# Loading experts' weights in 16 KB runs: the contraction index of each half matrix renamed

## The reference

```
t = RMSNorm(x) * ffn_norm_g                      # 256 x 1024
comb = softmax over the top 4 of 32 router logits # 256 x 32
for e in range(32):
    g = min(t @ w_gate[e] + b_gate[e], 7)
    u = clip(t @ w_up[e] + b_up[e], -7, 7)
    act = (u + 1) * (g * sigmoid(1.702 * g))
    out += comb[:, e] * (act @ w_down[e] + b_down[e])
```

## Time and profile before

| what | value |
|---|---|
| median of 3 runs | 1172.27 us |
| profiled execution: span, first to last instruction | 1169.7 us |
| TensorE matmul busy | 1102.9 us (94%) |
| TensorE weight load busy | 463.3 us (40%) |
| VectorE busy | 281.6 us (24%) |
| ScalarE busy | 190.4 us (16%) |
| bytes moved by DMA | 432.55 MB, 116,942 packets |
| mean DMA rate over the span | 370 GB/s |
| mean granted TensorE clock | 0.989 |

### The profile page before, as it was taken

The page is one execution under the profiler, slowest core; times in us unless marked ns, Lnnn a source line. Parts: engine busy times, 40 slices in busy tenths (PEclk is TensorE's granted clock), DMA queues, the critical chain, the costliest instruction groups (busy, mean ns, idle before and its releaser), DMA issues.

```text
span 1169.7 us, 13269 instructions
## 1 busy us (share of the span) xinstructions
PE 1102.9 (94%) x5385; PEld 463.3 (40%) x5385; DVE 281.6 (24%) x632; ACT 190.4 (16%) x361; POOL 62.6 (5%) x58
## 2 busy tenths in 40 slices
PE   6998998999999999999999999999999999999998
PEld 3787995333333333333333333333333333333332
DVE  4978664111111111111111111111111111111112
ACT  3645632100110010001000100001000100010000
POOL 0194120000000000000000000000000000000000
PEclk9989998999999999999999999999999999999999
DMA  8612478799999999999999999999999999999996
GB/s 314 256 73 108 171 295 334 293 402 409 409 409 409 410 409 409 409 410 410 409 409 410 410 409 410 409 410 410 409 409 410 410 410 409 410 410 409 409 409 259
DMA packets 116942, 432.55 MB, mean 370 GB/s; under 512 B 5557, under 2 KB 6106, under 8 KB 116922
## 3 DMA queue, kind: packets, MB, share of 16 engines
q1 hardware_dynamic: 116634, 431.60, 93.3%
q10 hardware_dynamic: 288, 0.67, 0.2%
HBM read 431.21 MB, written 1.05 MB: 370 GB/s over the span
## 4 chain that ended last, share of the span: by engine, by line
PE 48%; DMA 41%; DVE 7%; ACT 2%; SPq 1%; issue 1%; DVEq 0%; ACTq 0%
DMA ring<-in_exp_w_up 41%; PE ps L752 27%; PE ps L711 5%; PE ps L759 3%; PE ps L717 3%; PE ps L724 2%; PE ps L490 2%; PE ps L492 2%; PE ps L491 2%; DVE ring_r L1071 1%; DMA ring<-in_w_in 1%; SPq L434 1%; ACT ring_r L812 1%; DVE arena L1140 1%; DVE arena L1126 1%; PE ps L777 1%
## 5 line engine op out<-in xcount | busy, mean ns | idle before, releaser
L752 PE MATMUL ps<-ring,arena 128*64 128x512 f32 x3072 | 685.9, 594 | 32.5 <-DMA ring<-in_exp_w_gate 28.0
L752 PEld LDWEIGHTS ps<-ring,arena 128*64 128x64 f32 x3072 | 218.9, 137 | 486.8 <-issue 414.5
L1315 DVE TENSOR_SCALAR arena<-ps 128x512 f32<-128x512 f32 x32 | 22.1, 692 | 507.6 <-PE ps L752 507.6
L759 PE MATMUL ps<-arena 128*64 128x512 f32 x384 | 102.9, 614 | 0.3 <-issue 0.3
L1325 DVE TENSOR_SCALAR arena<-ps 128x512 f32<-128x512 f32 x32 | 22.1, 692 | 244.4 <-PE ps L752 244.4
L969 ACT COPY arena<-ps 128x512 f32<-128x512 f32 x32 | 18.8, 587 | 333.9 <-PE ps L711 333.9
L724 PE MATMUL ps<-arena 64*128 64x512 f32 x264 | 65.6, 615 | 0.8 <-ACT arena L975 0.8
L967 ACT ACTIVATE arena<-arena 128x512 f32<-128x512 f32 x32 | 20.1, 630 | 280.7 <-DVE arena L1315 280.7
L490 PE MATMUL ps<-ring_r 128*128 128x256 f32 (+1 forms) x192 | 61.1, 318 | 4.2 <-DVE ring_r L1071 2.4
L711 PE MATMUL ps<-arena 128*64 128x512 f32 x264 | 64.0, 607 | 0.8 <-DVE arena L1261 0.8
L975 ACT COPY arena<-ps 128x512 f32<-128x512 f32 x32 | 18.8, 586 | 249.0 <-PE ps L752 249.0
(11 more groups left out here) (185 smaller groups left out, 637.6 us busy)
## 6 DMA issues: line engine op xcount, KB each, us to landing
ring<-in_exp_w_gate SPq DMA_DIRECT2D x64, 2048.0 KB, 23.5
ring<-in_exp_w_up SPq DMA_DIRECT2D x64, 2048.0 KB, 23.7
ring<-in_exp_w_down SPq DMA_DIRECT2D x64, 2048.0 KB, 23.7
ring<-in_w_in SPq DMA_DIRECT2D x8, 2048.0 KB, 9.4
ring<-in_w_out SPq DMA_DIRECT2D x2, 2048.0 KB, 7.8
xt<-in_x SPq DMA_DIRECT2D x4, 512.0 KB, 6.9
ring<-in_pool_up SPq DMA_DIRECT2D x1, 2048.0 KB, 7.9
ring<-in_attn_up SPq DMA_DIRECT2D x1, 2048.0 KB, 8.6
```

Of the source, the lines that this page charges most:

```text
L752: last = mm(ps[BLOCK * half:BLOCK * (half + 1), bank, :], src[:, c, k % 2, :], slot(n)[:, c, HALF * half:HALF * (half + 1)], start=False, ...
L759: mm(ps[BLOCK * half:BLOCK * (half + 1), bank, :], this_e[:, buf, k, :], bias_rows[:, HALF * half:HALF * (half + 1)], start=True, stop=False)
L1315: v.tensor_scalar(g1, ps[:, 4, :], LIMIT, None, ALU.min).then_inc(g_ready, 1)
```

## The change

The contraction index of each half matrix is renamed: within a half of 512 rows, row 4 * p + c now belongs to partition p, block c. A partition's four rows are then neighbours in memory, one run of 16 KB. The bytes, the pieces, the slots, their order and their waits stay. To match it, VectorE writes `h2` and `act_out` with the same permutation of columns: it reads them in order, and writes neighbouring elements 128 elements (512 bytes) apart. Four of the `h2` writes and 32 of the `act_out` writes are concerned. The gain in the new order is loaded from HBM by one more DMA on ACT's queue (256 runs of 16 bytes), on a semaphore of its own, for which VectorE waits once before the loop. The router's part (`x2T`, `rw`, with the gain from `cols`) keeps the old order.

```diff
+        gain = sb("gain", [P, 2, 4])
...
+        gain_in = sem("gain_in")
...
-                        w = A[name][0].rearrange("e (c p) n -> p e c n", p=P)
+                        w = A[name][0].rearrange("e (h p c) n -> p e h (c n)", h=2, p=P)
...
-                            src = w[:, bass.ds(step * UNROLL + j, 1), 4 * half:4 * half + 4, :]
-                            src = src.rearrange("p e c n -> p (e c) n")
-                            sp.dma_start(slot(n), src).then_inc(slot_in[ORDER[n % SLOTS]], 16)
+                            src = w[:, bass.ds(step * UNROLL + j, 1), half:half + 1, :]
+                            src = src.rearrange("p e h n -> p (e h n)")
+                            sp.dma_start(ring[:, ORDER[n % SLOTS], :], src).then_inc(slot_in[ORDER[n % SLOTS]], 16)
...
             act.dma_start(con[:], consts).then_inc(con_in, 16)
+            act.dma_start(gain[:], A["ffn_norm_g"].rearrange("l (h p c) -> p (l h) c", h=2, p=P)).then_inc(gain_in, 16)
...
-                    v.tensor_scalar(h2[:, t, part_cols], xt[:, t, part_cols], rstd[:, t:t + 1], None,
+                    v.tensor_scalar(h2[:, t, part_cols].rearrange("q (c p) -> q p c", c=4),
+                                    xt[:, t, part_cols].rearrange("q (p c) -> q p c", c=4), rstd[:, t:t + 1], None,
                                     ALU.mult).then_inc(h2_ready, 1)
...
-                gain = cols[:, R_FFNG:R_FFNG + NC].rearrange("p (h c) -> p c h", h=2)
                 v.tensor_tensor(h_in[:, buf], ps[:, 6, :].rearrange("p (c h s) -> p c h s", c=4, h=2),
-                                wide(gain, [P, 4, 2, BLOCK], 3), ALU.mult).then_inc(h_in_ready, 1)
+                                wide(gain[:].rearrange("p h c -> p c h"), [P, 4, 2, BLOCK], 3),
+                                ALU.mult).then_inc(h_in_ready, 1)
+
+            dve.wait_ge(gain_in, 16)
...
-                        v.scalar_tensor_tensor(out=act_out, in0=u1, scalar=1.0, in1=gs, op0=ALU.add,
+                        v.scalar_tensor_tensor(out=act_out.rearrange("q (c p) -> q p c", c=4),
+                                               in0=u1.rearrange("q (p c) -> q p c", c=4), scalar=1.0,
+                                               in1=gs.rearrange("q (p c) -> q p c", c=4), op0=ALU.add,
                                                op1=ALU.mult).then_inc(act_ready, 1)
```

## The result

The changed kernel takes 1132.97 us (median of 4 runs, 1131.40 to 1134.66) against 1172.14 us: ratio 0.9669, 95% interval 0.9653 to 0.9684, so 39 us or 3.3% faster. The forecast was 1137.5 us, in a range from the floor of 1127.6 to the upper end of rival 1, 1160. The profiled execution has a span of 1132.4 us and a time of 1134.66, so an execution's time lies 2.3 us above its span.

A forecast was written before the change was run, and what follows sets the result against it. The DMA of expert weights was taken to bound the kernel (30.72 us an expert against TensorE's 28.45). After the change, DMA's side 1133.0 and TensorE's 1134.4 gave span 1135, plus 2.6: 1137.5 us, range 1127.6 to 1160.

The forecast's parts named there:

- rival 1: In the expert loop, the strided write costs TensorE's round 0.5 to 1.0 us: time 1143 to 1160 us, chance 0.17.
- The packet's fixed time: Expert weight stream: 9.0 ns fixed per DMA packet, so 16 KB runs save 0.215 us a piece, 39.6 us in all.
- TensorE's floor: Expert loop at 28.454 us an expert with the DMA out of the way: span 1124.6 us, nothing added to TensorE's round.
- The strided write: `act_out` in each expert takes 0.33 us longer, so TensorE's round grows by 0.26 us, 8.3 us over 32 experts.
- cover: After product 3, TensorE's `gather` hides 0.07 us of a longer `act_out`, no more.
- `h2`: Four strided writes before the expert loop, 1.03 us each instead of 483 ns: 1.1 us on the path.
- The gain's DMA: At the kernel's front, the added load's 256 small runs cost 0.4 us, bounds 0 and 1.0.
- The sum: Whole kernel: DMA's side 1133.0 us, TensorE's side 1134.4, span 1135, plus 2.6 from span to median: 1137.5.
- two bounds that would wait for each other: In the expert loop, DMA and TensorE, 1.4 us apart, would now and then wait for each other: span 1135.
- No effect on the stream: Expert weight loads stay at 409.6 GB/s, cut into 4 KB packets or not paying per packet: 1174 us, chance 0.12.
- Slower by the HBM side: Expert weight loads: partitions reading 16 KB apart lower the rate, 9.4 us per 1%, 1226 us at 388 GB/s; chance 0.08.
- TensorE as the bound: In the expert loop, TensorE becomes the bound by more than forecast, 3.2 us per 0.1 us of round; chance 0.17.

The follow-up runs named there:

- run 7: The changed kernel with the strided `act_out` instruction issued twice in each expert, the first time into a scratch place: 1163.50 us.
- run 5: The changed kernel with contiguous writes of `h2` and `act_out`, so the 16 KB loads alone: 1132.13 us.
- run 6: The changed kernel with `act_out`'s permutation moved to the PSUM reads of the g and u clamps, `h2` still strided: 1132.24 us, on a second run 1131.66 us.
- run 1: The changed kernel with each partition's 16 KB run fetched as 4 KB packets by two DMAs, same place in HBM: 1171.23 us, ratio 1.000 to the kernel before.

## Why the prediction was right, step by step

**The packet's fixed time: right, shown.** It was put at 9.0 ns from two rates of the trace of before; the long streams of 2, 8 and 16 KB give 9.4 each. The bounds of 5 to 12 ns were narrower than their stated source: the slices of 365 to 414 GB/s, put through the same two equations, give 20 and -2 ns. That the 8 us as a whole hit the value was in part luck. The stream took 904.5 us (211.80, its first issue, to 1116.3), forecast 902.5 and 3.0 of start. The page of the Trainium skill that has it at 3 cycles a packet (DMA: Bandwidth & Descriptors, "Why small descriptors are slow (HBM only)") gives the direction, not the size: between 4 and 16 KB the rate rose by 4.6%, not by the 1.7% that was estimated from it.

**TensorE's floor: right.** It was 1124.6 of span, with the last products 4 and 5 at 1110.6. They start at 1118.39, 7.8 later, and the parts are all in the rows: 0.2 because product 0 starts at 207.50 and not at 207.28, 0.3 because products 0 and 1 take 7.70 us and not 7.41, and 32 x 0.227 = 7.3 of the round. The middle one is the clock: from 205 to 210 us the granted clock is 0.60, against 0.68 in the kernel before, so more of that stretch runs at the lower of the two levels (1.2 GHz and not 2.4); in run 7, whose trace has 1.00 there, the two products take 6.87. 1124.6 and 7.8 make the span of 1132.4.

**The strided write: right in size, for a partly wrong reason.** It took 1053 ns against 1023 forecast from a strided read. The Trainium skill's note on SBUF "cachelines" (SBUF — State Buffer) has each access that crosses to a new line pay a penalty. For a write that was only argued. Runs 5 and 6 agree with it: it is the strided write into SBUF that costs, as 692 ns come back without it. The step in the round was to be 0.33 less a cover of 0.07, 0.26; it is 0.227, from two errors that nearly cancel. The instruction grew by 0.36, and the cover is 0.13. One wait shows it, that of the transposes' weight load for `act_out` (us in total, times, longest), in the kernel before and in the changed one:

```profile
PEld ps L717 <- DVE arena L1327: 26.0, 32, 0.8
```
```profile
PEld ps L719 <- DVE arena L1332: 33.5, 32, 1.1
```

That is 0.81 and 1.05 us each, 0.23 more, the whole step of the round; runs 5 and 6 have 26.0 again. I had read the cover from the start of the weight load to the end of `gather` (226.12 to 226.20). The weight load, however, started 0.18 us behind the end of `act_out` (225.94 to 226.12), and in the changed kernel 0.06 behind it:

```profile
225.76 1.05 DVE L1332 SCALAR_TENSOR_TENSOR arena<-arena 128x512 f32<-128x512 f32 x1
226.87 0.42 PEld L719 LDWEIGHTS ps<-con,arena 128*128 128x128 f32 x4 [1.04 <-DVE arena L1332]
226.87 0.66 PE L719 MATMUL ps<-con,arena 128*128 128x128 f32 x4 [0.17 <-DVE arena L1332]
```

So `act_out` could end some 0.12 us later at no price. Counted along the matmuls alone the step looks smaller at this place: from the end of product 3 to the transposes it is 1.85 us (225.02 to 226.87), where `gather` took 1.72. The rest is overlap that is lost. Before, the weight load ran beside the last matmul of `gather`, and the biases in front of products 4 and 5 took 1.01 us of the chain; now matmul and weight load start together at 226.87, and these biases take 1.08.

**`h2`: too dear.** Forecast 1.03 us each, measured 776 ns. From `h2` (now L1209) to the reduction behind it (now L1231), that is from 192.73 to 193.89, it is 1.16 us against 0.79, so 0.4 on the path and not 1.1. The slip is in the base: the sum took 1.07 ns an element from other instructions, though this instruction's own row stood at 483 ns. With that, 483 and 333 would have made 816. The price of the stride itself was 293 ns here and 360 for `act_out`, so one price per strided element fits both only roughly.

**The gain's DMA: not seen.** The front reaches this point at 192.73, the kernel before at 193.01. Executions differ there by some us: expert 0's products 4 and 5 start at 228.55, 229.28, in run 6 at 227.69 and in run 7 at 225.87, which is also about the spread of the runs. A term of 0.4 can't be read from one execution.

**The sum.** The 4.5 us between 1137.5 and 1132.97 are these. Of the span (1135 against 1132.4) there are 1.0 of start, since 1.5 were put in for `h2` and the gain and 0.5 came, 0.3 of it by the clock, 32 x 0.03 = 1.0 of the round, and 0.6 for two bounds that would wait for each other, which they don't while the DMA ends ahead of its need. The other 2.0 is the step from span to median, 2.6 in the kernel before and 0.6 here, since the profiled execution (1134.66) was the slowest of the four. That part is chance.

**The rivals.** No effect on the stream: refuted by 428.5 GB/s. Slower by the HBM side: refuted, and run 1 shows that the place as such does nothing either way at this pitch; no run has a larger one. TensorE as the bound: it is, by the price forecast and not more. Its 3.2 us for each 0.1 us of round held in run 7: 28.5 us for 0.89 by that price, and 30.0 in the medians beside the changed kernel on the same chip (1163.50 against 1133.46).

## What to carry to other kernels

Two steady stretches with different row sizes in one trace give the fixed time of a packet, and with it an estimate of the rate at other sizes; here 9 ns in 160 were 4.6% of the rate at 16 KB, and runs of 8 KB bring two thirds of that. Work out the next bound in the same sum, from the stretch in which it led before: it lay within 2 us of the new DMA time, so what is put on it by the way (the strided write) has to be priced as if it were exposed. A permutation that VectorE does on its way from PSUM was free here, the same one as a strided write to SBUF was not.

## What the runs showed of the hardware that wasn't expected

- The line of a fixed time plus bytes (9.4 ns a packet) holds from 2 to 16 KB; the prediction's 9.0 is within 0.3% of all four rates. Meanwhile the share shown for the DMA engines falls from 1.05 to 1.01 as packets grow.
- The place doesn't matter at these pitches: 4 KB packets flow at 410 GB/s whether a partition's four rows lie 512 KB apart or side by side (run 1).
- Splitting each 2 MB load into two of 1 MB on the same queue changes nothing (410 GB/s, ratio 1.000).
- Two strided VectorE instructions of 1.06 and 1.04 us in a row start 0.92 us apart, so they overlap by 0.14 us.
